# Conditioning products formed by GpSimd beside other stages, in a two-block transformer kernel

## The reference

```
mod = silu(c) @ ada_w[l] + ada_b[l]              # (1024) @ (1024, 6144)
sh1, sc1, g1, sh2, sc2, g2 = split(mod, 6)
h = x * (1 + sc1) + sh1
x = layer_norm(ALPHA * x + g1 * mixer(h))
h = x * (1 + sc2) + sh2
x = layer_norm(ALPHA * x + g2 * ffn(h))
```

## Time and profile before

| | us |
|---|---|
| median of 3 runs | 4279.76 (4278.24 to 4284.45) |
| the profiled execution | 4276.59 |
| its span | 4274.8 |
| busy: TensorE, VectorE, ScalarE, GpSimd | 3166.1, 2299.4, 1045.3, 932.1 |

### The profile page before, as it was taken

One profiled execution on the slowest core, in us unless ns is written; L12 is line 12 of the kernel. 1 busy time (PEld: TensorE's weight loads), 2 busy tenths in 40 slices (PEclk: granted clock), 3 DMA queues, 4 the chain that ended last, 5 costly groups with the idle time before them and its releaser, 6 DMA issues. The chain is left out here.

```text
span 4274.8 us, 37661 instructions
## 1 busy us (share of the span) xinstructions
PE 3166.1 (74%) x12012; PEld 1860.5 (44%) x12012; DVE 2299.4 (54%) x4802; ACT 1045.3 (24%) x2385; POOL 932.1 (22%) x804
## 2 busy tenths in 40 slices
PE   5767975977976868798777777777666664777776
PEld 1657933962734746233232232222264563322322
DVE  4456645746156338744665665555433648655554
ACT  1335422531232332111111111111232241111112
POOL 0000000000000012344444444444100023444442
PEclk9868997998986589999999999999987777999999
DMA  7214552536200111999999999999530034999996
GB/s 286 91 40 138 175 223 99 184 131 230 78 0 0 40 54 64 383 415 422 421 421 421 421 422 421 422 421 422 222 130 0 1 114 172 422 421 421 422 421 260
DMA packets 166466, 1052.95 MB, mean 246 GB/s; under 512 B 18332, under 2 KB 22172, under 8 KB 55344
## 3 DMA queue, kind: packets, MB, share of 16 engines
q0 software_dynamic: 110592, 805.36, 45.4%
q1 hardware_dynamic: 55728, 245.89, 16.0%
HBM read 1050.12 MB, written 1.05 MB: 246 GB/s over the span
## 5 line engine op out<-in xcount | busy, mean ns | idle before, releaser
L1800 PE MATMUL peer_fetch_summed<-peer_fetch_raw,peer_fetch_diag 128*128 128x512 f32 x3072 | 1443.4, 616 | 501.7 <-ACT peer_fetch_diag L1739 501.7
L1696 DVE CUSTOM_DVE_ANT_0 peer_fetch_raw<-peer_fetch_raw,peer_rows 128x1024 f32<-128x1024 f32 x768 | 940.2, 1225 | 852.6 <-DMA peer_fetch_raw<-in_peer_uv,peer_fetch_experts 852.1
L1800 PEld LDWEIGHTS peer_fetch_summed<-peer_fetch_raw,peer_fetch_diag 128*128 128x128 f32 x3072 | 567.2, 193 | 1368.7 <-ACT peer_fetch_diag L1739 777.4
L1618 POOL DMA_INDIRECT peer_fetch_raw<-in_peer_uv,peer_fetch_experts x768 | 855.6, 1114 | 1188.8 <-PE peer_fetch_summed L1800 1058.2
L1543 POOL TENSOR_TENSOR peer_keys_lo<-peer_pick_wq_raw,peer_keys_hi 128x1024 fp32r<-128x1024 f32 x32 | 76.3, 2389 | 2096.8 <-ACT peer_keys_hi L1502 2096.8
L1730 ACT ACTIVATE peer_fetch_gelu<-peer_fetch_score 128x2 f32<-128x2 f32 x384 | 78.1, 203 | 1629.2 <-DVE peer_fetch_score L1696 1629.2
L1739 ACT ACTIVATE peer_fetch_diag<-all_constants,peer_fetch_gelu 128x128 f32<-128x128 f32 x768 | 260.1, 386 | 0.5 <-issue 0.2
L124 PE MATMUL ffn_up_acc<-first_h_hi,ffn_up_hi 128*128 128x256 f32 x704 | 201.3, 286 | 36.9 <-DVE ffn_up_lo L644 36.9
L124 PE MATMUL ffn_up_acc<-first_h_lo,ffn_up_hi 128*128 128x256 f32 x704 | 200.9, 285 | 0.0
L124 PE MATMUL ffn_up_acc<-first_h_hi,ffn_up_lo 128*128 128x256 f32 x704 | 200.8, 285 | 0.0
L452 PE MATMUL mod_acc<-mod_weights,mod_act_c 128*1 128x512 f32 (+1 forms) x288 | 135.6, 615 | 43.9 <-DMA mod_weights<-in_ada_w 30.6
(11 more groups left out here) (483 smaller groups left out, 4808.0 us busy)
## 6 DMA issues: line engine op xcount, KB each, us to landing
mod_weights<-in_ada_w SPq DMA_DIRECT2D x48, 1024.0 KB, 7.4
in_up_raw<-in_w_up SPq DMA_DIRECT2D x88, 512.0 KB, 4.1
mod_weights<-in_w_mod SPq DMA_DIRECT2D x24, 1024.0 KB, 5.9
peer_fetch_next_raw<-in_w_mod SPq DMA_DIRECT2D x24, 1024.0 KB, 8.8
ffn_down_raw<-in_w_down SPq DMA_DIRECT2D x32, 704.0 KB, 5.6
peer_pick_wq_raw<-in_peer_wq SPq DMA_DIRECT2D x32, 512.0 KB, 3.3
peer_fetch_raw<-in_peer_uv,peer_fetch_experts POOLq DMA_INDIRECT x768, 19.0
in_in_raw<-in_ab_w_in SPq DMA_DIRECT2D x17, 512.0 KB, 3.4
```

Source lines behind the costliest of these rows:

```text
L1618: nc.gpsimd.indirect_dma_start(raw[:, n % ring].rearrange("p c d -> p (c d)"), None, uv_rows, bass.IndirectOffsetOnAxis(index[:, i, e:e + ...
L1696: nc.vector.tensor_tensor_reduce(raw[:, n % ring, 0, :], raw[:, n % ring, 0, :], rows[:, i, :], 1.0, 0.0, ALU.mult, ALU.add, score[:, i, e ...
L1800: ins = nc.tensor.matmul(summed[:, i % 2, half, :], diag[:, n % dring, :], raw[:, n % ring, 1, half * 512:(half + 1) * 512], start=(e == 0 ...
```

## The change

`mod0` makes only groups 0 to 3 (shift and scale of the first mixer) as before. The other 8 groups of it, the 12 of `mod1` and the 12 of `mod20` become 26 + 6 tasks of a new class `Quiet`, worked by GpSimd in four units each (a unit is two of the eight input chunks), beside stages in which GpSimd had nothing to do. GpSimd issues the weight load of each unit itself (512 KB, a ring of two), multiplies the raw weights by the conditioning column spread over 512, and adds both halves to a row of sums [128 partitions, 512]. Each instruction waits for the one before it. Later TensorE adds a finished row over the partitions (`collect`: for each 128 columns one matmul with the row as its weight and a column of ones), and VectorE adds the bias and the one (`settle`). Where the product has two columns, products and sums are made twice.

Units by stage, block one: projection 9, values 4, gates 2, decayed scores 6, head norm 3, window attention 6, output projection 4, layer norm 3, FFN up 27, FFN down 8 (these 72 with one column); pooling 8 with one column and 2 with two, layer norm 2, FFN up 15, FFN down 5 (with two). Block two, all with two: mLSTM 10, its norm 2, window attention 12. `collect` and `settle` stand in the split before the output projection (2 tasks), the layer norms (6, 10, 2, 4 tasks), FFN down of layer 1 (2), and in block two in the rotation (3) and the split (3). In the FFN, `hidden` shrinks from 22 slots to 2.

```diff
+class Quiet:
+    UNITS = 4
...
+    def fetch(self, pool, unit):
+        if unit >= self.UNITS * len(self.tasks):
+            return
+        job, g = self.tasks[unit // self.UNITS]
+        quarter = unit % self.UNITS
+        src = job["weights"][2 * g + quarter // 2][:, quarter % 2 * 2:quarter % 2 * 2 + 2]
+        pool.dma_start(self.ring[:, unit % self.slots], src).then_inc(self.s_loaded[unit % self.slots], 16)
+
+    def form(self, pool, count, spare=None):
+        if self.formed == 0:
+            for unit in range(self.slots):
+                self.fetch(pool, unit)
+        for unit in range(self.formed, self.formed + count):
...
+            raw = self.ring[:, slot]
+            pool.wait_ge(self.s_loaded[slot], 16 * (unit // self.slots + 1))
+            for j, mine in enumerate(self.place[task]):
+                scaled = raw if j == n - 1 else spare
+                scale = silu[:, quarter * 2:quarter * 2 + 2, j]
+                self.term.link(self.nc.gpsimd.tensor_tensor(scaled[:, 0:2, :], raw, bcast(scale, 512), ALU.mult))
+                if quarter == 0:
+                    self.term.link(self.nc.gpsimd.tensor_tensor(mine, scaled[:, 0, :], scaled[:, 1, :], ALU.add))
+                else:
+                    for i in range(2):
+                        self.term.link(self.nc.gpsimd.tensor_tensor(mine, mine, scaled[:, i, :], ALU.add))
+            self.fetch(pool, unit + self.slots)
+        self.formed += count
...
+    def collect(self, pe, tasks, acc, s_cols):
+        at = 0
+        for task in tasks:
+            for m in range(4):
+                for mine in self.place[task]:
+                    ins = self.nc.tensor.matmul(acc[:, at:at + 1], mine[:, m * P:(m + 1) * P], self.ones[:, 0:1], start=True, stop=True)
+                    at += 1
+        ins.then_inc(s_cols, 1)
...
 def layer_norm(...):
+            if quiet:
+                @block.gpsimd
+                def _(pool):
+                    quiet[0].form(pool, *quiet[1:])
...
+                if settle:
+                    keeper.collect(pe, tasks, cols, s_cols)
...
-            hidden = up.sb("hidden", [P, KF, T])
+            hidden = up.sb("hidden", [P, 2, T])
...
-        modulation(nc, "mod1", c, d["ada_w"][1], ada_b(1), mods, con("ident"))
...
-        modulation(nc, "mod20", c, d["w_mod"][0], bias(0), mods[0], con("ident"))
```

More of the change, by code:

```diff
@@ L142, in _ @@
                 ahead.start(sp)
+            if settle:
+                @block.tensor
+                def _(pe):
+                    quiet.collect(pe, tasks, cols, s_cols)
             @block.scalar
@@ L177, in start, with project @@
             self.fetch(sp, m, m, None)
-def project(nc, name, weights, kc, rhs, t, segments, loads=()):
+def project(nc, name, weights, kc, rhs, t, segments, loads=(), quiet=None, settle=None):
     with Stage(nc, name) as st:
@@ L410, in _, with modulation @@
                                          scale=gain[:, k:k + 1])
[L413 to L419 removed]
+def modulation(nc, name, sources, act_c, groups, weights, bias, mods, ident):
+    n = act_c.shape[2]
     half = KD // 2
     with Stage(nc, name) as st:
[L422 removed]
         wt = st.sb("weights", [P, 4, half, 512])
@@ L458, in _ @@
                 pe.wait_ge(s_row, groups)
-                for m in range(6 * KD):
+                for m in range(4 * groups):
                     ins = nc.tensor.transpose(cols[:, m, :], rows[:, m // 4, m % 4 * P:(m % 4 + 1) * P], ident[0:n, 0:n])
@@ L495, in _ @@
                 dve.wait_ge(s_cols, 1)
-                nc.vector.tensor_tensor(mods[:], cols[:], bcast(bias, n), ALU.add).then_inc(s_bias, 1)
+                nc.vector.tensor_tensor(mods[:, 0:4 * groups, :], cols[:], bcast(bias[:, 0:4 * groups], n), ALU.add).then_inc(s_bias, 1)
                 dve.wait_ge(s_bias, 1)
-                for first in (KD, 4 * KD):
-                    nc.vector.tensor_scalar(mods[:, first:first + KD, :], mods[:, first:first + KD, :], 1.0, None, ALU.add)
+                nc.vector.tensor_scalar(mods[:, KD:2 * KD, :], mods[:, KD:2 * KD, :], 1.0, None, ALU.add)
@@ L1235, in _, with mlstm @@
                     nc.scalar.activation(tmp[d][1][:], tmp[d][1][:], ACT.Ln, bias=1.0).then_inc(s_act, 1)
-def mlstm(nc, name, q, k, v, rows, u_cols, masks, select, ones, out):
+def mlstm(nc, name, q, k, v, rows, u_cols, masks, select, ones, out, quiet=None):
     with Stage(nc, name) as st:
@@ L1841, in offsets, with first_block @@
     return out, at
-def first_block(nc, d, x, vec, con):
+def first_block(nc, d, x, vec, con, silu, mods_2):
     with Stage(nc, "first") as blk:
-        mods = blk.sb("mods", [P, 6 * KD, 1])
+        mods = [blk.sb(f"mods{layer}", [P, 6 * KD, 1]) for layer in range(2)]
         h, z = blk.sb("h", [P, KD, T]), blk.sb("z", [P, KD, T])
@@ new lines, in first_block @@
+        tasks = [(layers[0], g) for g in range(4, 12)] + [(layers[1], g) for g in range(12)] + [(layers[2], g) for g in range(6)]
+        ring, sums = blk.sb("ring", [P, 2, 2, 512]), blk.sb("sums", [P, 10, 512])
+        spare = h.rearrange("p k t -> p (k t)").rearrange("p (u c) -> p u c", c=512)
+        quiet = Quiet(nc, blk, "quiet", ring, [sums[:, r, :] for r in range(10)], tasks, con("ones"))
+        modulation(nc, "mod0", [(silu[:, :, 0:1], c), (silu[:, :, 1:3], c_2)], silu[:, :, 0:1], 4, d["ada_w"][0], ada_b(0),
+                   mods[0], con("ident"))
@@ L1966, in peer_layer @@
                  con("iota"), con("ident"), upcoming)
-        modulation(nc, "mod20", c, d["w_mod"][0], bias(0), mods[0], con("ident"))
-        for layer, mixer in enumerate((mixer_ab, mixer_c)):
+        job = {"weights": d["w_mod"][0], "silu": silu[:, :, 1:3], "bias": bias(0), "mods": mods_2}
+        for layer in range(2):
             with Stage(nc, f"mix{layer}") as st:
@@ L1974, in second_block @@
                 modulate(nc, f"h2{layer}", h, pair, x, mods[layer], 0, (0, 1), ahead)
-                mixer(nc, d, ahead, h, pair, mods[layer], vec, con)
                 if layer == 0:
+                    quiet = Quiet(nc, st, "quiet2", h[:, 0:4].rearrange("p (u k) c -> p u k c", k=2), None,
+                                  [(job, g) for g in range(6, 12)], con("ones"))
+                    mixer_ab(nc, d, ahead, h, pair, mods[layer], vec, con, quiet)
                     with Stage(nc, "norm20") as norm:
```

221 lines of the change are left out of this document (167 added, 54 removed).

## The result

The changed kernel takes 4375.0 us (median of 4 runs, 4370.2 to 4382.5) against 4279.0 us of the kernel before beside it (4 runs, 4259.1 to 4284.5): ratio 1.0235, 95% interval 1.0198 to 1.0271. The forecast was 4390 us, the range 4225 to 4480. The profiled execution took 4382.5 us with a span of 4380.8, 106.0 more than before.

A forecast was written before the change was run, and what follows sets the result against it. Some seventy barrier-closed stages were taken to last as long as their slowest engine. From 4276.6 us, 216 removed, 325 given back by GpSimd's work and 5 for sums over partitions gave 4390.6, forecast 4390 us, range 4225 to 4480.

The forecast's parts named there:

- the lock: VectorE instructions with two SBUF inputs and GpSimd instructions reading SBUF exclude each other, the later waiting for the whole other.
- Part 1: Conditioning products: second and third stages go, the first keeps 4 of its 12 groups; 216 us removed.
- Part 2: GpSimd's cost per unit: product 2.39 us, 1.75 sums of 1.25, load issue 0.94, waits 0.2; 5.75 us in all.
- Part 3: Stages hosting units: even undisturbed, GpSimd's work outlasts them and the barriers wait for it; 113 us come back.
- Part 4: Stages hosting units: GpSimd and VectorE hold each other up, so their times add; 325 us given back in all.
- Part 4, FFN up: Both FFN up stages last GpSimd's time plus VectorE's 85 us of two-input work: 215 and 217 us, +80 and +83.
- Part 5: Sums over partitions: 176 one-column TensorE matmuls at 0.15 us, mostly hidden, with small VectorE additions; 5 us, bounds 3 and 12.
- Rival B: Stages hosting units: GpSimd waits for VectorE, never the reverse; 260 us given back, 4326 us in all; chance 0.22.
- Rival C: Stages hosting units: GpSimd's products stream beside VectorE, only the 113 us surplus comes back; 4179 us in all; chance 0.20.

The follow-up runs named there:

- the fills: Changed kernel with GpSimd's products and sums replaced by two zero fills each, which write SBUF but read none: 4162.4 us, ratio 0.9746 to the kernel before.

## Why the prediction was right

The sign, the size and the mechanism of the lock came out; how the lock makes the FFN up stages long was another way than the sum has it, and there the size is in part luck. By its steps:

- **Part 1**, removed 216 us: 216.8 (49.6 + 80.4 + 86.8), right.
- **Part 2**, the unit: 5.75 us forecast. The product with a spread column takes 1.91 us, not the 2.39 of the subtraction from which it was read the earlier trace rows, and an issue from GpSimd 0.59, not 0.94; the sum, 1.26, was right, and the waits between them are 0.45 for 0.2 (0.3 ahead of the issue, 0.02 to 0.08 ahead of the others). Undisturbed a unit takes 1.91 + 1.75 x 1.26 + 0.59 + 0.45 = 5.2 us. Both rows were of other instructions: same count of elements, but another output type; same engine, but an indirect load.
- The estimate by the Trainium skill ("GPSIMD Engine Reference", section 3.1, "Elementwise — side-by-side cycle accounting"), which has 4497 ns for a `tensor_tensor` addition over 2048 elements, was 1.33 us for 512 elements and 25 us more in the whole. The sums of this trace take 1.26, so it is 5% high here and the 25 us did not come.
- **Part 3**, the surplus: 113 us forecast, 66 by the fills. The fills of a set are some 0.35 us shorter than its product and sums (1.75 sums of 1.26 us against two fills of 0.53 for each), at most 62 us over the 176 sets, so the true surplus lies between 66 and 128, and this step isn't settled more closely. It contains what the sum put at nothing: GpSimd's wait at the end of a stage for the load that it issued last.
- **Part 4**, the lock: taken both ways, and shown both ways for VectorE's two-input instructions. The half that no row showed is now the run with fills: no reading, no delay of these. Most stages came out near their sums: FFN up +76 and +81 (forecast 80, 83), mLSTM +29 (27), scores +15 (15), first projection +10 (13), FFN down +0 and +4 (1, 7), the short ones +39 (36). Pooling, +39 for 49, is the cheaper unit: GpSimd is busy 58.9 us there, where I had 65.6 before any disturbance. So is window attention, +4 for 14: 104.8 us busy instead of 126, which fits. Together about 297 instead of 325, the sums over partitions in FFN down and one layer norm among them.
- **Part 4, FFN up**: its sum is for "a stage that GpSimd fills", and GpSimd does not fill it: it is done at 163.5 of 210.4 us. What costs is that nearly every delay of VectorE reaches TensorE at once, 2.3 to 2.8 us per unit from the first unit on; the same sum of holds and VectorE's time gave 142 and 135 us for 13 and 9 units, where 166.8 and 153.8 were measured. At 27 units the two accounts give nearly the same, and two errors inside the sum cancel: with the measured product the holds are 27 x 4.1 = 111 us instead of 124, and 20 us of `tensor_scalar` were not in it. VectorE was held for 81 us in this stage, GpSimd for some 22 (its products 2.13 us in the mean instead of 1.91, its sums 1.59 instead of 1.26).
- The Trainium skill's rule ("SBUF — State Buffer", "Who interferes with whom"), that the two engines exclude each other for whole instructions, holds for the two-input forms in every timeline read here, within 0.2 us. For GpSimd's one-input form this case measures less than the whole instruction (0.4 to 0.7 of 1.56 us). The same section also names `tensor_scalar` among the forms that can take both of VectorE's ports and then contend with GpSimd, which the prediction left out. The trace agrees: the `tensor_scalar` of 0.41 us grew to 1.32 in the mean.
- **Part 5**, the sums over partitions: 5 us forecast, bounds 3 to 12; about 22 by the runs, 20 of them in stages that have nothing else new. This step failed, by size and by cover. One takes 0.32 us, since an f32 matmul is two instructions; the row for it was there, 0.23 for one instruction of the layer norm, which also has two per matmul (16 for 8), and I had gone towards the transposes. At 40 of them 12.6 us lie behind the last matmul that the stage needs, and the digestion that was to cover them lasts some 7.6.
- Beyond the steps some 6 us are in the fetching and other stages.

So 4390.6 less 28 for the stages and 1 for what was removed, plus 15 for the sums over partitions and 6 for the rest, is 4383, the profiled execution's time: errors that cancel in part. Rival B is excluded by the subtractions of up to 3.08 us. Rival C failed on the 213 us that lie between fills and products, of which at most 62 are the fills' shorter time.

## What to carry to other kernels

An idle engine is not free capacity: before work is moved to GpSimd, count VectorE's instructions with SBUF inputs in the host stage and how close its consumer follows, since each unit there costs about what it delays VectorE, from the first unit on. Price each place per unit against what the unit costs where it is now (here 1.55 us against 0 to 4), and move only to the cheap ones. Where GpSimd may end a stage last, don't let it issue a load just ahead of the barrier: here that was 4 to 5 us each time. Take f32 matmuls as two instructions each, however few columns they have, and put those that nobody needs soon before the wait of a stage and not behind its last matmul.

## What the runs showed of the hardware that was not expected

- VectorE's `tensor_scalar` over 256 elements, with one SBUF tensor as input, is held up by GpSimd: 0.41 us alone, 0.73 in the mean beside fills, which read nothing, and 1.32 beside products. Instructions with an input in PSUM kept 0.41. In the trace of before a `tensor_scalar` from SBUF to SBUF takes 1.23 us for 2048 elements (L354), as long as a subtraction of two SBUF tensors takes for 1024.
- GpSimd's drain at the end of a stage lasts until the load that it issued last has landed, 4.0 to 5.4 us for 512 KB.
- A GpSimd `tensor_scalar` with a scalar column takes 1.56 us for 512 elements, and a `tensor_tensor` with the column spread 1.91 for 1024: the one-input form is the dearer one, and disturbs VectorE less.
- A fill of 1024 elements takes GpSimd 0.95 us, one of 512 0.53, and the issue of a direct load of 512 KB 0.53 to 0.59.
